# Scalings of the scan moved up, the experts' gate product split from the up product, three weight loads moved behind the fetched rows

## The reference, cut to what matters

```
# the scan, in chunks of 128 tokens, per direction
xdt = (x * dt[..., None])
y_diag = einsum(cb * decay_in, xdt)
states = einsum(Bh * exp(cs[-1:] - cs), xdt)          # state at the end of each chunk
final, entering = lax.scan(step, init, ...)           # carry * decay + state
y_off = einsum(Ch, entering) * exp(cs)

# the experts
expert = top 2 of the 8 experts of the best of 4 groups, per token
hid = silu(einsum('td,edf->tef', t, w_gate)) * einsum('td,edf->tef', t, w_up)
out = einsum('tef,efd->td', hid * combine, w_down)
```

## Time and profile before

| what | value |
|---|---|
| median of 3 runs | 1518.5 us |
| the profiled execution's own time | 1518.79 us |
| its span, first to last instruction | 1516.9 us |
| PE busy | 1274.4 us, 84% |
| DVE, ACT, POOL busy | 457.0, 326.0, 163.7 us |
| DMA | 339.63 MB, mean 224 GB/s |
| granted TensorE clock, mean | 0.927 of 2.4 GHz |

### The profile page before, as it was taken

How to read it: one execution, slowest core, us unless ns; L and a number is a source line. 1 busy time by engine, 2 the same in 40 slices (tenths; PEclk the granted TensorE clock), 3 DMA queues, 4 the chain that set the end, 5 groups by cost and what they waited for, 6 DMA issues and landing times.

```text
span 1516.9 us, 14684 instructions
## 1 busy us (share of the span) xinstructions
PE 1274.4 (84%) x5389; PEld 646.0 (43%) x5389; DVE 457.0 (30%) x974; ACT 326.0 (21%) x830; POOL 163.7 (11%) x242
## 2 busy tenths in 40 slices
PE   3899879899998888995998887299988959987881
PEld 1465544555545555443333332154455443333330
DVE  0115458533235553033111011401266241111014
ACT  3212456201110000022111011412255231111013
POOL 1000012100000001001111110207000111211101
PEclk9999989899999999996999999599999979999896
DMA  9974400276930013424899999915040557999993
GB/s 332 367 275 176 156 28 1 93 281 222 369 113 0 1 56 114 187 83 154 357 397 420 420 419 400 323 68 58 12 161 10 207 215 302 395 419 421 419 384 140
DMA packets 94457, 339.63 MB, mean 224 GB/s; under 512 B 12752, under 2 KB 16534, under 8 KB 69697
## 3 DMA queue, kind: packets, MB, share of 16 engines
q1 hardware_dynamic: 71296, 296.89, 50.1%
q0 software_dynamic: 16208, 35.02, 7.7%
q10 hardware_dynamic: 6897, 6.97, 1.3%
HBM read 336.62 MB, written 23.18 MB: 237 GB/s over the span
## 4 chain that ended last, share of the span: by engine, by line
PE 59%; DMA 15%; DVE 9%; issue 3%; ACT 3%; SPq 0%; POOL 0%; ACTq 0%; DVEq 0%; POOLq 0%
PE bank L744 54%; DMA ring<-in_moe_w_up_dram 13%; PE bank L748 4%; PE bank L775 1%; DMA arena<-expert_rows 1%; DMA expert_rows<-arena,scr 1%; DVE rstd L1992 1%; DVE arena L2139 0%; DVE arena L2141 0%; DVE rstd L1989 0%; ACT ring L1698 0%; DMA hT<-rows,scr 0%; DVE xR L2143 0%; DVE arena L1994 0%; DVE arena L1990 0%
## 5 line engine op out<-in xcount | busy, mean ns | idle before, releaser
L744 PE MATMUL bank<-ring,arena 128*64 128x512 f32 (+3 forms) x2016 | 493.7, 578 | 63.7 <-DMA ring<-in_moe_w_up_dram 51.6
L744 PEld LDWEIGHTS bank<-ring,arena 128*64 128x64 f32 (+1 forms) x2016 | 185.1, 152 | 322.2 <-issue 308.9
L744 PE MATMUL bank<-hT,ring 128*128 128x384 f32 (+1 forms) x896 | 299.3, 495 | 6.4 <-ACT hT L1376 6.4
L744 PEld LDWEIGHTS bank<-hT,ring 128*128 128x128 f32 (+1 forms) x896 | 171.8, 193 | 131.9 <-issue 14.2
L744 PE MATMUL bank<-arena 128*64 128x32 bf16 (+8 forms) x656 | 125.9, 403 | 25.2 <-DVE arena L1994 15.2
L2114 DVE TENSOR_TENSOR hT<-hT,bank 128x256 f32<-128x256 f32 x32 | 13.5, 421 | 310.2 <-ACT hT L1586 310.2
L744 PEld LDWEIGHTS bank<-arena 128*128 128x128 f32 (+4 forms) x656 | 71.6, 173 | 71.9 <-issue 41.7
L748 PE MATMUL bank<-cst,arena 128*128 128x128 f32 (+3 forms) x207 | 35.8, 337 | 64.3 <-ACT arena L1363 41.7
L748 PEld LDWEIGHTS bank<-cst,hT 128*128 128x128 f32 x368 | 48.4, 193 | 63.4 <-issue 49.1
L1586 ACT ACTIVATE hT<-bank 128x256 f32<-128x256 f32 x32 | 12.3, 383 | 291.7 <-PE bank L744 291.7
L748 PE MATMUL bank<-cst,hT 128*128 128x128 f32 x368 | 62.2, 305 | 13.6 <-DMA hT<-rows,scr 12.1
(11 more groups left out here) (280 smaller groups left out, 1107.9 us busy)
## 6 DMA issues: line engine op xcount, KB each, us to landing
ring<-in_moe_w_gate_dram SPq DMA_DIRECT2D x30, 2048.0 KB, 16.9
ring<-in_moe_w_up_dram SPq DMA_DIRECT2D x30, 2048.0 KB, 21.5
ring<-in_moe_w_down_dram SPq DMA_DIRECT2D x30, 2048.0 KB, 22.9
ring<-in_w_ada_dram SPq DMA_DIRECT2D x24, 2048.0 KB, 14.7
ring<-in_ev_w_in_dram SPq DMA_DIRECT2D x11, 2048.0 KB, 11.6
ring<-in_ev_w_out_dram SPq DMA_DIRECT2D x4, 2048.0 KB, 18.9
ring<-in_od_w_in_dram SPq DMA_DIRECT2D x3, 2048.0 KB, 15.9
arena<-expert_rows POOLq DMA_DIRECT2D x6, 1024.0 KB, 7.1
```

The source lines that it names most:

```text
L744: return nc.tensor.matmul(out, lhsT, rhs, start=start, stop=stop_, skip_group_check=True)
```

## The change

Scan, DVE: the scaling of a chunk state stands directly behind line 1898 of its step, ahead of `weigh` and of the taking of y; decaying and adding the states 2 and 3 (now `enter_state`) stays at the end of the step. Experts: `gate_up` computes all of the gate product, then all of the up product, each of 16 matmuls of 256 columns (before, 16 of 512 columns made both); the gate product waits for its own weights alone and counts a semaphore of its own (`g_done`), on which SP's next gate load waits. Layer 0's end: all six loads of the next weights wait for the third piece of fetched rows.

```diff
@@ -673,7 +673,7 @@
                 for part in parts:
-                    sp.wait_ge(S("gu_done%d" % l) if part < 2 else S("down_done%d" % l), gone)
+                    sp.wait_ge(S(("g_done%d", "gu_done%d", "down_done%d")[part] % l), gone)
                     sp.dma_start(halves(expert_part(s, part)), expert_source(l, pair, part)).then_inc(S("efull%d_%d" % (l, 3 * s + part)), 16)
@@ -721,8 +721,7 @@
                 sp.wait_ge(S("down_done0") if s % 3 == 2 else S("gu_done0"), gone)
-                if k >= n1 + 3:
-                    sp.wait_ge(S("yg%d" % (NT - 1)), 16)
+                sp.wait_ge(S("yg%d" % (NT - 1)), 16)
                 static_load(k, True)
@@ -1131,20 +1130,19 @@
                 def gate_up(n, b):
                     rs = ring_set(n, b)
-                    for part in range(2):
-                        expert_full(pe, l, n, rs, part)
                     pe.wait_ge(s["x_act"], n + 1)
                     pe.wait_ge(s["x_dve"], n + 1)
                     if not (isinstance(n, int) and n < 2):
                         pe.wait_ge(s["hid"], n - 1)
                     x = xsT[:, b, :].rearrange("p (k m) -> p k m", k=KD)
-                    two = area(6144, 2 * SLOT) if rs is None else ring[:, 3 * rs * SLOT:(3 * rs + 2) * SLOT]
-                    w = two.rearrange("p (x e k n) -> p e k x n", x=2, e=2, n=HID)
-                    for k in range(KD):
-                        for e in range(2):
-                            o = banks[2 + b][e * CAP:(e + 1) * CAP, :].rearrange("p (x n) -> p x n", x=2)
-                            last = mm(o, x[:, k, e * CAP:(e + 1) * CAP], w[:, e, k, :, :], k == 0, k == KD - 1)
-                    last.then_inc(s["gu_done"], 1)
+                    for part, ready in enumerate(("g_done", "gu_done")):
+                        expert_full(pe, l, n, rs, part)
+                        w = expert_part(rs, part).rearrange("p (e k n) -> p e k n", e=2, n=HID)
+                        for k in range(KD):
+                            for e in range(2):
+                                last = mm(banks[2 + b][e * CAP:(e + 1) * CAP, part * HID:(part + 1) * HID],
+                                          x[:, k, e * CAP:(e + 1) * CAP], w[:, e, k, :], k == 0, k == KD - 1)
+                        last.then_inc(s[ready], 1)
@@ -1859,8 +1857,8 @@
                    over(wsc[:, t, d, :], HDIM), mult).then_inc(S("xw"), 1)
-                if i < 2:
-                    return
+
+            def enter_state(d):
                 src, dst, t = ((0, 1, 1), (3, 2, 2))[d]
@@ -1900,6 +1898,8 @@
                         TT(ct, ct, over(xbcT[:, KD + 2 + q // 2, tt], 4, False), mult).then_inc(S("ctd"), 1)
+                if STATE_AFTER.get(step):
+                    chunk_state(STATE_AFTER[step])
                 if q == 3 and t + 1 < NT:
@@ -1911,8 +1911,8 @@
                 take(TT(szT[:, 2 * q:2 * q + 2, tt], szT[:, 2 * q:2 * q + 2, tt], ps, mult))
-                if STATE_AFTER.get(step):
-                    chunk_state(STATE_AFTER[step])
+                if STATE_AFTER.get(step, 0) >= 2:
+                    enter_state(STATE_AFTER[step] - 2)
```

More of the change, by code:

```diff
@@ L1114, in moe @@
                 s = {x: S("%s%d" % (x, l)) for x in
-                     ("x_ps", "x_act", "x_dve", "gu_done", "hid", "ht_done", "ht_act", "down_done", "d_act", "d_dve")}
+                     ("x_ps", "x_act", "x_dve", "g_done", "gu_done", "hid", "ht_done", "ht_act", "down_done", "d_act", "d_dve")}
                 def turn(n, b):
```

## The result

| | us, median (lowest to highest, runs) | ratio to before, 95% interval |
|---|---|---|
| before | 1519.1 (1518.1 to 1522.1, 4) | |
| changed | 1498.4 (1497.0 to 1500.6, 4) | 0.9862 (0.9843 to 0.9881) |
| forecast | 1502.0 (1497 to 1510) | |

The change gains 20.7 us between the medians, where 16.6 were forecast; the profiled executions are 18.1 apart (span 1498.8 for 1516.9). The time lies in the range. Each ratio in this document is to runs of the kernel before that were made beside it, with medians of 1519.1 to 1520.5 us.

A forecast was written before the change was run, and what follows sets the result against it. The prediction took the PE's own work and the stream of expert weights as the bounds. Scan 6.0, loads behind the rows 4.2 and split 6.4 us sum to 16.6, from 1518.5 to 1502 us, range 1497 to 1510.

The forecast's parts named there:

- Scan, 6.0 us forecast: Scan: moving three scalings ahead removes the PE's waits at xw; 6.0 us, ends 3 and 7.1.
- the walk: Scan steps timed in the new order: y of step 3 starts at 218.8 instead of 225.33, 6.5 us.
- Rival 5: Experts: shorter idle times keep the clock at 2.4 GHz and the tails gain too; 1497 us, 2%.
- Rival 2: Scan: another wait, on ACT's exponentials or POOL's product, leaves 2 us of 6; 1506 us, 8%.
- Loads behind the rows, 4.2 us: Layer 0's end: without the next loads beside it, the last store takes 2.64 us, not 6.80; ends 3 and 4.5.
- The cover of 9 us: Layer 1's start: first weights land at 975.1, while the first product waits for ACT's input until 984.06.
- What the split costs, nothing: Experts' gate_up: 64 matmul records for 32 cost nothing; upper end 2.6 us a turn.
- rivals 1, 3 and 4: Split: 1, a pair takes 0.25, 1508, 13%; 3, weights don't load beside matmuls, 1520, 4%; 4, halves run serially, 1644, 3%.
- Rival 3: Experts: weights don't load beside matmuls, each added pair pays up to 0.165 us, 2.6 a turn; 1520 us, 4%.
- What the split gives, 2.8 us a layer: Experts: gate 3 is issued 3.5 us earlier into an idle stream; the last load lands 2.8 us earlier.
- The layout: Experts: a layer's 39 loads timed in order; 0.8 us lost near 750 us, from there the stream is full.
- The tail of layer 0, 0.8 us: End of layer 0's experts: half of gate_up is done before, so the last product waits for its load alone; 0.8 us.

The follow-up runs named there:

- the filled kernel: The kernel before with 12 constant 128x128 matmuls in each of the PE's three idle times ahead of the scan's states 1 to 3: 1517.5 us, ratio 0.9995.
- the longer fillers: The changed kernel with the PE's idle times in the routing ahead of each layer's experts filled with 24, 10 and 36 constant matmuls: 1497.4 us, ratio 0.9856.
- e9: The kernel before with the scan change and the loads behind the rows, but without the split: 1506.6 us, ratio 0.9911.
- e5: The changed kernel with its new order of products, but every expert gate load waits for both products of its turn: 1506.3 us, ratio 0.9918.

## Why the prediction was right, and where it was not

- **Scan, 6.0 us forecast.** The mechanism was right: no idle time before the states, one before y of step 2 and one before the last state, 1.18 and 0.39 us for 0.6 and 0.6. The size was wrong: 8.9 us in the stretch, where the walk gave 6.5 and the range ended at 7.1; 9.5 by the medians. The step that failed is "The stretch crosses changes of the clock ... so I take 6.0": the walk kept the clock of before (exponents of step 2 at 3.0 us, measured 1.88; y of step 3 at 218.8, measured 216.6). Removing idle time took the slow stretches with it, 1.7 us each, as the filled kernel shows. Rival 5 named this mechanism, but for the experts and with 2%. Rival 2 fell.
- **Loads behind the rows, 4.2 us.** Right to 0.1: 6.80 - 2.67 = 4.1, in the kernel with this part alone 4.1 too (6.80 - 2.70). The cover of 9 us was 9.8 (first weights landed at 958.8, product at 968.60). By the estimate that the prediction made from the Trainium skill's turn-taking between queue rows (DMA: Bandwidth & Descriptors, "Queues, rings and completion order"), a store at worst doubled, it would have been 3.4. The trace disagrees with that estimate: 6.80 is 2.5 times 2.67.
- **What the split costs, nothing.** Right: 7.13 us for 7.09, and rivals 1, 3 and 4 fall by the same row. Rival 3 was also a rule of the Trainium skill (TensorE: Matmul & The Clock Gate, "The mechanism"), by which a weight load overlaps only matmuls of another group of rows; the row of 7.13 us disagrees. The 0.04 us stand midway between nothing and the estimate of 0.08 that the prediction took from the Trainium skill's gap of 2.5 ns (the same page, "Back-to-back issue gap").
- **What the split gives, 2.8 us a layer.** The size was right, 2.9 and 2.7 between means, though 2.2 and 1.6 in the first pair of profiles. A step behind it was wrong: "Other gate loads go out 3.5 us earlier as well, but behind full queues that is worth nothing." With only the first two early, the streams are 2 to 3 us longer. The layout lost 0.8 us near 750 us and then called the stream full; it is not full for three turns more. The later loads, put at nothing, keep 0.7 to 3.8 us a layer by themselves, and the first ones, put at 2.8, between nothing and 1.5: that the two errors offset each other is luck.
- **The tail of layer 0, 0.8 us.** Wrong: the last product starts 1.7 us after its weights (932.49, landed 930.75), before 1.1; so 0.6 us are lost. The down product ahead of it took 5.37 us at a low clock, 3.65 in the turns at full clock. What I took from the layout as a gain of waits went to the clock.
- **The sum.** In the two profiled executions the terms measure 8.9 us (scan), 2.2 and 1.6 (streams), -0.6 (tail) and 4.1 (store), 16.2 for the 16.6 forecast. That the sum came out is luck in part: the scan gave 2.9 more, streams and tail 3.2 less. Another 1.9 us, to the 18.1 between these executions, lie where no part of the change is: 1.0 between the scan and layer 0's experts, 0.6 between layer 0's last store and layer 1's experts, 0.3 behind layer 1's stream. The medians are 20.7 apart; the 2.6 more I can lay to no one part, and that stays open.

## What to carry to other kernels

Cost an idle time of the PE at its own length and, where long products follow, at the products run at half the clock as well; look at the granted clock behind each wait that a change removes. A stream that is full on average may have empty queues in its first turns: there each release is worth its time, so lay out issue and landing of each load until its latency from issue stays above that of a lone load. Where nothing can be done sooner, harmless matmuls in the idle time buy the clock, but count their length from a trace: the longer fillers, which overran in both layers, gave most of it back (1497.4 us for 1491.8).

## What the runs showed that I had not expected

- **The split keeps the clock up in the experts.** Stretches of 150 us (765 to 915), of the changed kernel, then of the kernel with no split (e9):

```profile
765.12:915.12 150.00, 124.69 (x892) 69.99 (x888) 18.05 (x30) 18.52 (x40) 24.30 (x40) 0.99 1.01 418
```

```profile
765.00:915.00 150.00, 124.53 (x540) 47.96 (x538) 16.24 (x27) 16.71 (x37) 24.38 (x40) 0.91 1.01 418
```

  Timeline of the PE there, without the split:

```profile
857.45 9.92 PE L743 MATMUL bank<-ring,arena 128*64 128x512 f32 x32 [3.99 <-DMA ring<-in_moe_w_up_dram]
```

  and with it, all gate loads late (e5):

```profile
845.44 3.65 PE L743 MATMUL bank<-ring,arena 128*64 128x512 f32 x16 [1.49 <-DMA ring<-in_moe_w_down_dram]
...
850.95 3.67 PE L743 MATMUL bank<-ring,arena 128*64 128x256 f32 x32 [1.42 <-DMA ring<-in_moe_w_gate_dram]
856.09 3.67 PE L743 MATMUL bank<-ring,arena 128*64 128x256 f32 x32 [1.46 <-DMA ring<-in_moe_w_up_dram]
```

  One wait of 4 us for both weights has become several of 1.4, and no product behind them is slow. It costs or gives no time here (1506.3 us for e5, 1506.6 for e9), since the stream is the bound (419 and 418 GB/s). A kernel bound by its PE may gain by it; no run here shows that.
- **Small float32 matmuls as fillers are dear.** One of 128x128 has two records and took 0.115 to 0.123 us a record at full clock (24 in 2.94 us, 72 in 8.3), 0.23 to 0.25 a matmul; I had planned with half of that, and in all three kernels that used them some overran.
